# A two-layer decoder step on one core: samples between the prompt heads in the attention, the bias in its natural order, and the samples' compressed values in the scores' bank

## The reference, cut to what matters

```python
def _attn_probs(q, k, qpos, kpos, rel_bias, mask):
    logits = jnp.einsum('bqhgd,bkhd->bhgqk', q, k).astype(jnp.float32) * (HEAD_DIM ** -0.5)
    bias = rel_bias.astype(jnp.float32)[_rel_bucket(qpos[:, None] - kpos[None, :])]
    ...
    p = jax.nn.softmax(jnp.where(mask, logits + bias, NEG_INF), axis=-1)
    return jnp.where(mask, p, 0.0)

def _nsa_layer(h, ckv, ...):            # ckv: keys and values of compressed blocks
    hn = _rmsnorm(h, norms_l[0])
    proj = hn @ w_q_l                   # 16 heads of 128, and three gates per head
    p_c = _attn_probs(q, ckv[:, :, 0], qpos, kpos_c, rel_bias, kpos_c[None, :] <= qpos[:, None])
    o_c = jnp.einsum('bhgqk,bkhd->bqhgd', p_c, ckv[:, :, 1])
    sel = _select_blocks(p_c, qpos, n_slc)
    o_s = sel_fn(q, sel)                # selected blocks
    o_w = win_fn(q)                     # sliding window
    o = gates[:, :, 0] * o_c + gates[:, :, 1] * o_s + gates[:, :, 2] * o_w
    h = h + _rmsnorm(o.reshape(B, S, -1) @ w_o_l, norms_l[1])
    return _ffn_sublayer(h, norms_l, w_in, w_out)
```

## Time and profile before

| | |
|---|---|
| time, median of three runs | 2627.52 us (2627.11 to 2628.7) |
| the profiled execution | 2632.45 us |
| its span, first to last instruction | 2630.8 us |
| mean granted clock of TensorE | 0.989 |

### The profile page before, as it was taken

One profiled execution on the slowest core, in us unless ns is written; L12 is line 12 of the kernel. 1 busy time (PEld: TensorE's weight loads), 2 busy tenths in 40 slices (PEclk: granted clock), 3 DMA queues, 4 the chain that ended last, 5 costly groups with the idle time before them and its releaser, 6 DMA issues.

```text
span 2630.8 us, 44401 instructions
## 1 busy us (share of the span) xinstructions
PE 2548.2 (97%) x17502; PEld 2486.9 (95%) x17502; DVE 1223.7 (47%) x1384; ACT 909.8 (35%) x1124; POOL 282.9 (11%) x316
## 2 busy tenths in 40 slices
PE   8799999999999999999999989999999999999997
PEld 6799999999999999999996779899999999999997
DVE  6664444444444444643535633644444444444444
ACT  3354333322322333522323533533233223323332
POOL 2430000000000001300002311300000000000012
PEclk9899999999999999999999989999999999999998
DMA  6524444444444444444462354344444444344443
GB/s 250 177 96 149 153 161 149 149 155 156 156 147 166 149 143 152 139 150 152 144 227 91 120 186 144 128 136 144 161 160 149 148 162 153 135 166 160 143 151 127
DMA packets 82203, 400.26 MB, mean 152 GB/s; under 512 B 8188, under 2 KB 18812, under 8 KB 52194
## 3 DMA queue, kind: packets, MB, share of 16 engines
q1 hardware_dynamic: 81570, 390.06, 43.0%
q0 software_dynamic: 576, 9.47, 1.0%
HBM read 391.80 MB, written 15.82 MB: 155 GB/s over the span
## 4 chain that ended last, share of the span: by engine, by line
PE 85%; DVE 6%; ACT 3%; SPq 2%; issue 2%; DMA 2%; POOL 1%; ACTq 0%; DVEq 0%
PE ps L1259 27%; PE ps L1261 27%; PE ps L1260 27%; ACT w_hi L464 1%; DVE w_lo L710 1%; PE ps L1350 1%; SPq L349 1%; DMA w_raw<-w_out_dram 1%; PE ps L1437 1%; DVE winB L817 1%; DVE winA L817 0%; DMA pastK<-win_k_dram 0%; ACT y L572 0%; ACT x_hi L490 0%; PE ps L1509 0%
## 5 line engine op out<-in xcount | busy, mean ns | idle before, releaser
L1259 PE MATMUL ps<-x_hi,w_hi 128*128 128x320 f32 x3536 | 1096.1, 310 | 7.0 <-DVE sg L881 4.1
L1260 PE MATMUL ps<-x_lo,w_hi 128*128 128x320 f32 x3536 | 1094.3, 309 | 0.0
L1261 PE MATMUL ps<-x_hi,w_lo 128*128 128x320 f32 x3536 | 1094.2, 309 | 0.0
L710 DVE TENSOR_TENSOR w_lo<-w_raw,w_hi 128x2048 fp32r<-128x2048 f32 (+1 forms) x365 | 751.3, 2059 | 657.0 <-ACT w_hi L464 657.0
L464 ACT CAST w_hi<-w_raw 128x2048 fp32r<-128x2048 f32 (+1 forms) x365 | 624.6, 1711 | 532.9 <-PE ps L1261 472.7
L1259 PEld LDWEIGHTS ps<-x_hi,w_hi 128*128 128x128 f32 x3536 | 665.3, 188 | 9.1 <-DVE sg L881 4.6
L1260 PEld LDWEIGHTS ps<-x_lo,w_hi 128*128 128x128 f32 x3536 | 665.3, 188 | 0.2
L1261 PEld LDWEIGHTS ps<-x_hi,w_lo 128*128 128x128 f32 x3536 | 665.2, 188 | 0.0
L1259 PE MATMUL ps<-hid_hi,w_hi 128*128 128x320 f32 x1408 | 435.3, 309 | 0.8 <-DVE w_lo L710 0.8
L1261 PE MATMUL ps<-hid_hi,w_lo 128*128 128x320 f32 x1408 | 435.1, 309 | 0.0
L1260 PE MATMUL ps<-hid_lo,w_hi 128*128 128x320 f32 x1408 | 435.1, 309 | 0.0
(11 more groups left out here) (240 smaller groups left out, 1534.1 us busy)
## 6 DMA issues: line engine op xcount, KB each, us to landing
w_raw<-w_in_dram SPq DMA_DIRECT2D x176, 1024.0 KB, 4.9
w_raw<-w_out_dram SPq DMA_DIRECT2D x128, 704.0 KB, 4.1
w_raw<-w_kv_dram SPq DMA_DIRECT2D x24, 1024.0 KB, 4.9
w_raw<-w_q_dram SPq DMA_DIRECT2D x17, 1024.0 KB, 4.9
w_raw<-w_o_dram SPq DMA_DIRECT2D x16, 1024.0 KB, 4.9
win_out_dram<-win_kv_dram POOLq DMA_DIRECT2D x8, 992.0 KB, 5.3
rowsK<-cmp_data_dram SPq DMA_DIRECT2D x16, 256.0 KB, 9.2
w_raw<-w_pool_dram SPq DMA_DIRECT2D x4, 1024.0 KB, 6.8
```

The lines of the kernel that those rows point to most:

```text
L710: V.tensor_tensor(w_lo[:, slot, 0:width], w_raw[:, slot, 0:width], w_hi[:, slot, 0:width].bitcast(F32), ALU.subtract).then_inc(lo_made, 1)
L1259: M(out, wh, xh[:, k, :], start=(k == 0), stop=False)
L1260: M(out, wh, xl[:, k, :], start=False, stop=False)
L1261: last = M(out, wl, xh[:, k, :], start=False, stop=(k == kt - 1))
```

## The change

The prompt heads and the samples are put in another order: after every two heads comes a sample. Position `p` in the loop is unit `unit(p)`. The samples' keys and values have one buffer each, in LO alone, so HI holds the bias for the whole loop. The bias is no longer loaded reversed and flipped: the row of each head is repeated 128 times, DRAM to DRAM, by eight transfers on POOL's queue, and SP loads it with a shift of one element per partition in natural order, in two halves. The one-hot product moves into the K/V projection. The K/V output is stored in eight parts, one behind each sample's loads. The order of the setup changes, and copies of values move from VectorE to ScalarE. A sample's compressed scores are one product over 60 columns for the four key/value heads at once (a mask keeps the own head's), and its compressed values go into the last 128 columns of its scores' bank. The outputs of all units alternate between banks 6 and 7. The second panel of the output projection is loaded into `w_rawY`, a part of the query's place, while the loop runs.

```diff
+    def unit(p):
+        b, k = divmod(p, 3)
+        return NH + b if k == 2 else 2 * b + k
+    def place(u):
+        return 3 * (u - NH) + 2 if u >= NH else 3 * (u // 2) + u % 2
...
 # SyncE
-        sp.dma_start(kv_out[:, :, :], kvT[:, :, :]).then_inc(rows_out, 16)
+        t = bias_dram.tensor
+        sp.wait_ge(trow_out, 16 * (NH // 2))
+        sp.dma_start(bias_s[:, :], bass.AP(t, DS - 1, [[P * NL, NH], [NL - 1, DS], [1, PAST + DS]])).then_inc(bias_s_in, 16)
+        def bias_half(n):
+            h0 = n * (NH // 2)
+            sp.dma_start(biasP[:, bias_at(h0):bias_at(h0) + NH // 2, :],
+                         bass.AP(t, h0 * P * NL + PAST + DS - 1 - P, [[NL - 1, P], [P * NL, NH // 2], [1, SEQ]])).then_inc(bias_in, 16)
         sp.wait_ge(lo_made, P_WO)
         sp.dma_start(w1Kp[:, :, :], cmp_w1[0]).then_inc(w1Kp_in, 16)
-        sp.wait_ge(trow_out, 16)
+        sp.wait_ge(tile_made, P_WO - 1 + TOFF)
+        bias_half(0)
         sp.wait_ge(tile_made, P_WO + TOFF)
-        sp.dma_start(revP[:, :, :], bass.AP(t, DS, [[1, P], [NE, NH], [1, SEQ]])).then_inc(rev_in, 16)
+        bias_half(1)
         def load_keys(b):
-            if b >= 2:
-                sp.wait_ge(s_made, NH + b - 1)
+            if b:
+                sp.wait_ge(s_made, place(NH + b - 1) + 1)
...
         def load_values(b):
-            if b >= 2:
-                sp.wait_ge(o_made, NH + b - 1)
+            if b:
+                sp.wait_ge(o_made, place(NH + b - 1) + 1)
...
+        for b in range(DB):
+            load_keys(b)
+            load_values(b)
+            part = slice(b * N_KVT // DB, (b + 1) * N_KVT // DB)
+            sp.dma_start(kv_out[:, part, :], kvT[:, part, :]).then_inc(rows_out, 16)
+            if b == 0:
+                sp.wait_ge(crow_sum, 2)
+                panel(P_WO, 0, w_o[0], PW)
+            if b == DB // 2:
+                sp.wait_ge(s_made, place(PW // NT) + 1)
+                sp.dma_start(w_rawY[:, :], w_o[1]).then_inc(raw_in[(P_WO + 1) % 2], 16)
 # ScalarE
+        def copy_vP(n):
+            act.wait_ge(vt_sum, n + 1)
+            nc.scalar.copy(vP[:, n // 2, n % 2, :], ps[:, 4 + n, :]).then_inc(vt_made, 1)
         gelu(2, 1, hcP[:, 1, :])
+        copy_vP(0)
+        copy_vP(1)
         gelu(3, 0, hcP[:, 0, :])
+        copy_vP(2)
+        copy_vP(3)
+        act.wait_ge(kc_sum, 3)
+        nc.scalar.copy(vCP[0:NCMP, :], ps[0:NCMP, 4, :]).then_inc(vcp_made, 1)
...
             if s == UNITS:
-                act.wait_ge(s_made, UNITS)
+                act.wait_ge(s_read, place(NH // 2 - 1) + 1)
                 hi_split(P_WO, 0)
+            if s == UNITS + 1:
+                act.wait_ge(s_read, UNITS)
+                hi_split(P_WO + 1, 0, src=w_rawY[:, :])
 # VectorE, setup; the eight copies of flipped bias are gone
+        dve.wait_ge(mask_set, 1)
+        dve.wait_ge(bias_s_in, 16)
+        V.tensor_copy(bias_n[:, DB - 1, :], bias_s[:, PAST:PAST + DS])
+        for v in range(NKV):
+            rows = slice(32 * v, 32 * v + 32)
+            V.tensor_copy(biasSC[rows, v * NCMP:(v + 1) * NCMP], bias_s[rows, CB - 1:PAST:CS])
+        dve.wait_ge(bias_in, 32)
...
+        crow_copy(1, 0)
+        cmp_join(3, 2, NKV, False)
 # VectorE, scores of a sample
-            link(V.scalar_tensor_tensor(out=o[:, 0:NCMP], in0=ps[:, a, W:W + NCMP], scalar=SCALE,
+            link(V.scalar_tensor_tensor(out=o[:, 0:NC4], in0=ps[:, a, W:W + NC4], scalar=SCALE,
                                         in1=biasSC[:, :], op0=ALU.mult, op1=ALU.add))
+            if b >= 2:
+                dve.wait_ge(o_made, place(NH + b - 2) + 1)
+            V.tensor_copy(vC[:, b % 2, :], ps[0:NC4, a, 512 - HD:512])
...
 # GpSimd
+        pool.dma_start(row_dram[:, :], trow[:, 0:NL]).then_inc(row_out, 16)
+        pool.wait_ge(row_out, 16)
+        for n in range(NH // 2):
+            pool.wait_ge(tile_made, P_KV + TOFF + 8 + 2 * n)
+            pool.dma_start(bias_dram[2 * n:2 * n + 2, :, :], rep(row_dram[2 * n:2 * n + 2, :], P)).then_inc(trow_out, 16)
 # TensorE, setup
+        pe.wait_ge(w1Vp_in, 16)
+        crow_part(1, w1Vp, 0, CS).then_inc(crow_sum, 1)
+        pe.wait_ge(w1Kp_in, 16)
+        crow_part(0, w1Kp, 0, 6)
+        turn_sums(0, 1)
         pe.wait_ge(sig_made, 1)
         # the gates, as before
+        crow_part(0, w1Kp, 6, CS).then_inc(crow_sum, 1)
+        turn_values(0)
+        turn_values(1)
+        turn_sums(1, 0)
+        pe.wait_ge(gates_made, 1)
+        turn_values(2)
+        turn_values(3)
         pe.wait_ge(cmp_hid, 4)
+        M(ps[:, 3, 0:NKV * NCMP], w2[:, 0, :], hcP[:, 0, :], start=True, stop=True).then_inc(kc_sum, 1)
         pe.wait_ge(kc_made, 2)
 # TensorE, a sample
-            pe.wait_ge(pastK_in[b % 2], 48 * (b // 2 + 1))
+            pe.wait_ge(pastK_in, 48 * (b + 1))
...
+            M(ps[:, a, PAST + NEW:PAST + NEW + NC4], qS[:, b, :, :].rearrange("p h i -> p (h i)"),
+              kcS[:, b * NC4:(b + 1) * NC4], start=True, stop=True)
+            M(ps[0:NC4, a, 512 - HD:512], hcS[:, 1, b * NC4:(b + 1) * NC4], w2[:, 1, :],
+              start=True, stop=True).then_inc(s_made, 1)
...
+            M(ps[:, bank, 0:HD], t[0:NC4, 768:896], vC[:, b % 2, :], start=False, stop=True).then_inc(o_made, 1)
 # the loop
             if s < UNITS:
                 scores(s)
-            if s >= NH + 4:
-                turn_outputs(s - 4 - NH)
+            if s == 0:
+                compressed_values()
+            if s == 1:
+                new_values()
+            if s == 2:
+                pe.wait_ge(vcp_made, 1)
+                pe.wait_ge(vt_made, 5)
+            if is_sample(s - 4):
+                turn_outputs(s - 4)
```

More of the change, by code:

```diff
@@ L420, in _ @@
[L420 to L436, removed]
+                sp.dma_start(pastV[:, 0, p, :], slc_kv[page(b * NPG + p), :, 1, :]).then_inc(pastV_in, 16)
@@ L456, in _, with hi_split @@
         A = nc.scalar.activation
-        def hi_split(c, half, width=PW):
+        def hi_split(c, half, width=PW, src=None):
             slot = c % 2
+            src = w_raw[:, slot, 0:width] if src is None else src
             act.wait_ge(raw_in[slot], half * 16 + 16 * (c // 2 + 1))
@@ L463, in hi_split @@
                 act.wait_ge(tile_made, tiles_before(c - 1, half))
-            nc.scalar.copy(w_hi[:, slot, 0:width], w_raw[:, slot, 0:width]).then_inc(hi_made, 1)
+            nc.scalar.copy(w_hi[:, slot, 0:width], src).then_inc(hi_made, 1)
         def tile_wait(c, half):
@@ L649, in exps, with copy_p, out_high @@
             last.then_inc(exp_made, 1)
[L651 to L657, removed]
+        def copy_p(p):
+            act.wait_ge(t_made, p + 1)
+            if p >= 2:
+                act.wait_ge(o_made, p - 1)
+            nc.scalar.copy(pT[:, p % 2, 0:512], ps[:, 4, :]).then_inc(pTa_made, 1)
+        def out_high(p):
+            u, bank = unit(p), 6 + p % 2
             if u < NH:
-                act.wait_ge(o_made, u + 1)
-                nc.scalar.copy(x_hi[:, u, 0:SEQ], ps[:, out_bank(u), 0:SEQ]).then_inc(ohi_made, 1)
+                act.wait_ge(o_made, p + 1)
+                nc.scalar.copy(x_hi[:, u, 0:SEQ], ps[:, bank, 0:SEQ]).then_inc(ohi_made, 1)
             else:
@@ L1211, in _ @@
         last.then_inc(qS_made, 1)
-        for u in range(UNITS):
-            s3 = u % 3
-            pool.wait_ge(rec_made, u + 1)
+        for p in range(UNITS):
+            s3 = p % 3
+            pool.wait_ge(rec_made, p + 1)
             o, f = sc[:, s3, :], rec[:, s3, :]
-            if u < NH:
+            if not is_sample(p):
                 v = pick(o, 0, 272, 2, NCMP)
@@ L1558, in transposes @@
-            for v in range(NKV):
-                o_ = (b * NKV + v) * NCMP
-                last = M(ps[0:NCMP, 7, v * HD:(v + 1) * HD], hcS[:, 1, o_:o_ + NCMP], w2[:, 1, :], start=True, stop=True)
-            last.then_inc(vc_sum, 1)
-        def outputs(u):
-            pe.wait_ge(pTa_made, u + 1)
-            pe.wait_ge(pTb_made, u + 1)
-            if u >= 2:
-                pe.wait_ge(o_read, u - 1 if u < NH else u)
-            p = pT[:, u % 2, :]
+            T(ps[:, 5, 0:P], o[:, 64 + PAST:64 + PAST + 2 * NEW], ident)
@@ L1569, in outputs @@
+            T(ps[0:NC4, 5, 256:384], o[:, 0:NC4], ident).then_inc(t_made, 1)
+        def outputs(p):
+            u, bank = unit(p), 6 + p % 2
+            pe.wait_ge(pTa_made, p + 1)
+            pe.wait_ge(pTb_made, p + 1)
+            if p >= 2:
+                pe.wait_ge(o_read, p - 1)
+            t = pT[:, p % 2, :]
             if u < NH:
                 v = slice((u // GQ) * HD, (u // GQ + 1) * HD)
-                O = ps[:, out_bank(u), 0:SEQ]
-                M(O, vP[:, 0, 0, v], p[:, 0:256], start=True, stop=False)
@@ L1590, in outputs @@
             for n in range(NKV):
                 v, O = head(n)
[L1592 to L1601 removed]
+                M(O, t[:, 512 + 32 * n:544 + 32 * n], vN[:, v], start=False, stop=False)
```

339 lines of the change are left out of this document (148 added, 191 removed).

## The result

The change made the kernel 0.3% slower: 2635.22 us (median, 2631.67 to 2639.95) against 2628.04 us (2627.11 to 2630.73), seven runs each, ratio 1.0026 with a 95% interval of 1.0016 to 1.0035. 2613.0 was forecast. The profiled execution took 2633.92 us, its span is 2632.4. That is 1.5 us above the profiled execution of before, where the medians are 7.2 apart: the profiled one of before was itself 4.4 us above the median given here, and behind the stage that follows it took 1080.1 us (2630.8 - 1550.67) where the one of after took 1077.7, over the same tiles. So what the traces are compared on is the stage alone.

The account below looks back on a forecast made before the run. TensorE was to set the heads, late keys the rounds: 1400.6 + 22.1 + 96.7 + 16.8 = 1536.2 against 1550.67, a gain of 14.5 us from the 2627.5 median, so 2613.0; likeliest case's range 2606 to 2620.5.

Parts of the forecast that it names:

- first scores: End of the setup: the first prompt scores were to start at 1400.6, a gain of 11.8 us.
- stretch to the second sample: From the first scores to the second sample's scores: five passes, four heads and one sample, 22.1 us.
- six rounds: From the second sample's scores to the last one's: five rounds of 15.7 us and one of 18.2, 96.7 in all.
- the end: From the last sample's scores to the output projection: 16.8 us, at most 23.3.
- The wait that I expect: In the loop, TensorE waits for keys queued behind values: 3.9 + 11.8 = 15.7 us a round, 2.0 above the engines' need.
- 3.9 us after that pass began: In a sample's pass, when the previous sample's outputs end: 1.3 of scores, about 1.0 of transposes, 1.57 of outputs.
- first parts: From a sample's scores to SP's issue of that sample's values: 4.75 us in the prediction's terms, 28.5 over six rounds.
- at a wash: In the samples, the compressed values' single product and the wider score columns were to cost TensorE nothing net.
- the keys would never be late: Rival for the loop: loads land in time and engines set 13.7 us a round, 2598.5 us in all; chance 0.14.
- the two kinds of unit don't overlap: Rival for the loop: samples' waits hold the heads, 17.5 us a round at worst, 2621.3 us in all; chance 0.13.
- the third rival: DRAM-to-DRAM copies on POOL's queue hold up the weight panels and TensorE stands: 2653 us in all; chance 0.07.
- second parts: From SP's issue of a sample's values to the next sample's scores: 10.95 us, 13.45 with the panel, 68.2 over six.

Follow-up runs that it names:

- ones and late output: Changed kernel with eight products of ones before a sample's wait for keys and the K/V output's eight parts stored behind the loop: 2611.65 us, ratio 0.9935.
- ones in the wait: Changed kernel with eight extra TensorE products of ones before each wait for keys from the third sample on, queue order kept: 2621.36 us, ratio 0.9969.
- keys first: Changed kernel with the next sample's keys issued ahead of the current sample's values in SP's queue: 2597.85 us; with the DRAM-to-DRAM copies also spread, 2597.84 us.
- four versions in the table: Changed kernel with ones before the key waits (2621.4 us), K/V output behind the loop (2616.0), both edits (2611.7), or next keys ahead of values (2597.9).
- the copies spread: Changed kernel with the eight DRAM-to-DRAM copies written with the 128 rows outermost in place of the two heads: 2632.35 us, ratio 1.001.
- the output late: Changed kernel with the eight K/V output parts issued behind all samples' loads, no longer between values and keys: 2615.98 us, ratio 0.995.

## Why the prediction was wrong

The ledger of the stage, from its start to the output projection: 1536.2 was predicted, 1554.69 came, 18.5 later. The first scores were right (1400.48 for 1400.6). The stretch to the second sample was 2.4 us shorter than reckoned (19.74 for 22.1); the sum took full passes, and the first ones have nothing to transpose or to output yet. The six rounds were 17.6 longer (114.3 for 96.7), the end 3.4 longer (20.2 for 16.8).

**The step that failed** is the term of "The wait that I expect" that puts the end of the outputs "3.9 us after that pass began". Of the 17.6 us in the rounds 14.7 are in the first parts (43.2 for 28.5) and 2.9 in the second (71.1 for 68.2); the 11.8 us for SP's part were nearly right (11.9 in the first round, 1425.10 to 1436.98). The 3.9 fell short in two ways.

One is a size. In the first round, at 1.00, it is 4.88 us. Transposes (1.03) and outputs (1.64) take what was reckoned, but from the scores to the transposes pass 2.21 us (1420.22 to 1422.43), not 1.3. The prediction left the product of the compressed values "at a wash" and out of the 3.9. In the trace of the kernel before it already lies on that stretch, from 1510.86, between the transposes and the outputs:

```profile
1511.53 0.31 PE L1589 MATMUL ps<-pastV,pT 128*32 128x128 f32 x3
...
1513.28 1.07 PE L1519 MATMUL ps<-pastK,qS 128*32 128x256 f32 x16
```

That pass took 4.61 us from its scores to the end of its outputs (1508.67 to 1513.28) at 1.00, and the prediction had the row to see it. In the changed kernel the product and the wider score product begin at 1421.44, and 0.20 us of wait for POOL ends the piece. With ones and late output, where all six rounds run at 1.00, the first parts take 32.9 us for the 28.5: some 0.7 us a round, 4.4 in all.

The other is a mechanism that the sum didn't have. Behind each wait for the keys, 3.0 to 5.9 us here, the granted clock is down, and the 87 products that follow run slowly (7.44 us at 0.58 in the third round). They are just those that SP's values wait for, and the keys stand behind the values: a late key makes the next key later. This is shown by the ones in the wait, with the queue as it was: the same 87 products at 1.00 in 4.69 us, 13.9 us less in all, 8.3 of them in the stage as traced; and by keys first, which removes the wait itself and finds 1.00 everywhere. By the first parts it is about 10 us of the 14.7 (43.2 less the 32.9 at 1.00), and the 3.4 of the end too: with less or nothing to wait for, or with ones in the wait, four versions in the table end in 16.7 us. That this is the predicted 16.8 is in part luck: from the last outputs to the projection pass 3.35 us (1551.34 to 1554.69) where 4.76 were reckoned, and what lies ahead of them takes 13.4 for 12.05 in those four.

The Trainium skill, "TensorE: Matmul & The Clock Gate", section "HAM oscillation — how this bites in real kernels", describes a matmul kernel in which each step's wait for a load sends the array back to the lower clock, so that every step starts cold and pays anew. This case's trace agrees (five of the six rounds, and the end, hold stretches below 1.00), with one thing more: here the slow products also delay the load that the next step waits for.

**The rivals.** That the keys would never be late was wrong for this queue, but its 13.7 us and 2598.5 are what keys first measures (13.67 and 2597.85). That term came out right in part by luck: TensorE works 13.5 us a round where the prediction had 12.9, the product left out of it among them, and the 0.8 us of new wait is 0.2. That the two kinds of unit don't overlap is out by the same run. The copies from DRAM to DRAM were slow, as the third rival said, and cost little, if anything: with the copies spread it is 2632.35 us for 2635.22, 0.1%, close to the noise, and with keys first there is no difference. The prediction's rule of the Trainium skill on the outermost dimension ("DMA: Bandwidth & Descriptors", Rules for kernel authors) agrees with 15.6 against 4.4 us. The same edit cut the packets of that queue from 5744 to 1008 between 1000 and 1600 us, so the runs don't say which of the two shortened the copies.

One sum of the prediction is off: the terms that it names for the upper end of its range (16.6 us a round, a panel at 4.0, setup 1.5 later) add to 2621.4, not 2620.5, if the panel's round grows like the others. The measured time lies beyond both.

**What stays open.** The medians rose by 7.2 us, the stage in the profiled executions by 3.7; 2.4 of the rest is the slower remainder of the profiled execution of before. How the second parts divide between SP's issue and landing was not measured by itself, nor why keys are issued more slowly right behind an output.

## What to carry to other kernels

When an in-order queue holds loads for two consumers, put first the load whose buffer comes free first: here keys b+1 behind values b cost 37 us, and swapping them removed every wait for keys. Price a new wait on TensorE with what it does to the products behind it: here they took 7.44 us for 4.88, and if a buffer is freed at their end, the wait feeds the next one. A product that is a wash on an engine's busy time still counts in a chain that it lies on; look at which event it precedes.

## What the runs showed that was not expected

In the changed kernel two loads of key pages were issued in 2.62 to 2.91 us right behind an output part; in the rounds with the output late, with none ahead of them, it was 1.9 (once 2.24). In the panel's round, where the panel stands between the output part and the keys, it was 1.88 too. What slows the issue is not shown. And eight products that compute nothing, 1.9 us in each round, made the kernel 13.9 us faster.
